# Projecting the dilated values of two chunks between the norm's chunks, with their weights sent among the chunks of x

## The reference

```
def rmsnorm(x, g):
    y = xf * lax.rsqrt(jnp.mean(xf * xf, axis=-1, keepdims=True) + RMS_EPS)
    return (y * g).astype(x.dtype)

def even_mixer(hn, w_in, b_f, w_out, dil_slopes):
    zq, zk, zv, zf, dq, dk, dv = split_cols(hn @ w_in, EVEN_SPLIT)
    log_f = jax.nn.log_sigmoid((zf + b_f).astype(F32)).transpose(0, 2, 1)
    ...
    o_b = dilated_attention(to_heads(dq, 8), to_heads(dk, 8), to_heads(dv, 8), dil_slopes)
    ...

for layer in range(2):
    h = h + mixer(rmsnorm(h, attn_norm[layer]), ...)
    h = h + hierarchical_moe(rmsnorm(h, ffn_norm[layer]), ...)
return rmsnorm(h, final_norm)
```

## Time and profile before

| | us |
|---|---|
| median of 3 runs (lowest to highest) | 1088.04 (1087.25 to 1089.6) |
| span of the profiled execution | 1087.8 |
| PE busy | 999.3 (92%) |
| DVE busy | 387.4 (36%) |
| ACT busy | 228.5 (21%) |
| POOL busy | 91.0 (8%) |
| PE's share of the chain of waits | 66% |
| transfers' share of that chain | 21% |

### The profile page before, as it was taken

The page is one execution under the profiler, slowest core; times in us unless marked ns, Lnnn a source line. Parts: engine busy times, 40 slices in busy tenths (PEclk is TensorE's granted clock), DMA queues, the critical chain, the costliest instruction groups (busy, mean ns, idle before and its releaser), DMA issues.

```text
span 1087.8 us, 12861 instructions
## 1 busy us (share of the span) xinstructions
PE 999.3 (92%) x5140; PEld 575.7 (53%) x5140; DVE 387.4 (36%) x1103; ACT 228.5 (21%) x573; POOL 91.0 (8%) x102
## 2 busy tenths in 40 slices
PE   5999999999998999999778999989999999998866
PEld 3344644455465656666434647536455666665532
DVE  3123721345145333222235217448225333222215
ACT  3113620236021000000012216437111100000002
POOL 2000000000101011111101001000100111111100
PEclk9999999999999999999999999999999999999999
DMA  9522105965336999999999320023634799999996
GB/s 317 213 109 78 78 2 175 211 271 184 115 115 237 406 421 419 420 419 419 419 371 340 156 78 1 11 78 155 239 115 169 283 423 418 420 419 420 418 395 250
DMA packets 64125, 276.95 MB, mean 255 GB/s; under 512 B 12851, under 2 KB 17443, under 8 KB 39994
## 3 DMA queue, kind: packets, MB, share of 16 engines
q1 hardware_dynamic: 53808, 257.48, 61.3%
q0 software_dynamic: 10256, 18.64, 4.9%
HBM read 261.94 MB, written 30.44 MB: 269 GB/s over the span
## 4 chain that ended last, share of the span: by engine, by line
PE 66%; DMA 21%; DVE 5%; issue 4%; SPq 3%; POOL 1%; ACT 0%; POOLq 0%; DVEq 0%
PE bank L855 13%; PE bank L946 10%; PE bank L1069 9%; PE bank L867 9%; DMA K<-rows,small 9%; PE bank L886 6%; PE bank L1083 4%; DMA D<-in_moe_w_down 4%; DMA hnT<-in_moe_w_down 3%; PE bank L900 3%; PE bank L1262 2%; PE bank L916 2%; DMA expert_rows<-K,small 1%; PE bank L980 1%; SPq L454 1%
## 5 line engine op out<-in xcount | busy, mean ns | idle before, releaser
L855 PE MATMUL bank<-hnT,W 128*128 128x512 f32 x336 | 145.1, 593 | 0.8 <-ACT hnT L1356 0.8
L1083 PE MATMUL bank<-D,PT 128*64 128x512 f32 x416 | 102.2, 594 | 10.6 <-DMA D<-in_moe_w_down 9.9
L855 PEld LDWEIGHTS bank<-hnT,W 128*128 128x128 f32 x336 | 63.7, 190 | 80.4 <-issue 79.3
L1069 PE MATMUL bank<-W,PT 128*64 128x256 f32 x640 | 79.0, 388 | 12.4 <-DMA W<-in_moe_w_up 4.9
L1781 DVE SCALAR_TENSOR_TENSOR PT<-bank,small,PT 128x256 f32<-128x256 f32 x32 | 15.5, 484 | 202.6 <-PE bank L1069 202.6
L1803 DVE SCALAR_TENSOR_TENSOR K<-K,small,bank 128x512 f32<-128x512 f32 x64 | 47.8, 747 | 91.8 <-PE bank L1083 91.6
L1069 PE MATMUL bank<-W,cst 128*64 128x256 f32 x640 | 77.2, 380 | 1.8 <-DMA W<-in_moe_w_up 1.8
L1388 ACT ACTIVATE P<-P,nm 128x128 f32<-128x128 f32 (+5 forms) x128 | 68.4, 537 | 30.1 <-DVE nm L1575 29.7
L886 PE MATMUL bank<-K,Q 128*128 128x256 f32 (+3 forms) x256 | 70.4, 417 | 2.2 <-DVE nm L1575 1.0
L867 PE MATMUL bank<-W,hnT 128*128 128x512 f32 (+2 forms) x256 | 71.8, 440 | 0.0
L1069 PEld LDWEIGHTS bank<-W,PT 128*64 128x64 f32 x640 | 52.0, 138 | 32.1 <-issue 12.1
(11 more groups left out here) (241 smaller groups left out, 1358.4 us busy)
## 6 DMA issues: line engine op xcount, KB each, us to landing
D<-in_moe_w_down SPq DMA_DIRECT2D x48, 1024.0 KB, 20.2
W<-in_moe_w_gate SPq DMA_DIRECT2D x40, 1024.0 KB
W<-in_moe_w_up SPq DMA_DIRECT2D x36, 1024.0 KB, 19.9
hnT<-in_moe_w_down SPq DMA_DIRECT2D x12, 1024.0 KB, 17.7
W<-in_e_w_in SPq DMA_DIRECT2D x5, 2048.0 KB
expert_rows<-K SPq DMA_DIRECT2D x2, 4096.0 KB, 34.6
V<-in_moe_w_gate SPq DMA_DIRECT2D x6, 1024.0 KB
Q<-in_moe_w_gate SPq DMA_DIRECT2D x6, 1024.0 KB
```

Of the source, the lines that this page charges most:

```text
L855: last = nc.tensor.matmul(b[:, :], w[:, k, 128 * fb:128 * fb + 128], hnT[:, k, :], start=(k == 0), stop=(k == KD - 1))
L1069: last = nc.tensor.matmul(bank[b][at, 0:256], XT[k // 4][:, k % 4, at], w[:, 256 * k:256 * k + 256], start=(k == 0), stop=(k == KD - 1))
L1083: last = nc.tensor.matmul(bank[5 + half][at, :], hT[:, 128 * c + 64 * a:128 * c + 64 * a + 64], d[:, col:col + 512], start=(c == 0), stop= ...
```

## The change

SP's queue now sends the gain ahead of the small table, and the value weights W2 in two halves of 256 columns, one behind chunk 0 of x and one behind chunk 1. W0 follows whole, then the masks, W1 and W3; W2's old load is gone. POOL issues its three small loads behind the norm, ahead of the position rows. TensorE transposes chunk 0, projects its first 256 value columns, transposes chunk 1, projects the other 256, transposes chunks 2 and 3 and projects the values of chunk 1. The queries follow. The first scores come straight behind the keys, and two value groups follow them. ScalarE and VectorE copy in the new order; ScalarE warms its root with another operand, so that it waits for the table only ahead of the first root; the scratch of the first squares moves from V to P.

```
         junk = flatV[:, 0:1024]
+        first_junk = P[:, 1, 0:1024]
...
         def _(sp):
+            def load_value_half(half):
+                sp.dma_start(W[2][:, :].rearrange("p (k n) -> p k n", k=KD)[:, :, 256 * half:256 * half + 256],
+                             ewin_v[:, :, EVEN_COLS[2] + 256 * half:EVEN_COLS[2] + 256 * half + 256])\
+                  .then_inc((s_half, s_ld["W2"])[half], (16, 48)[half])
             for c in range(C):
                 sp.dma_start(h[:, c, :], x[0, 128 * c:128 * c + 128, :]).then_inc(s_x[c], 16)
                 if c == 0:
-                    sp.dma_start(cst[:, 0:C_MASKS], const_table[:, 0:C_MASKS]).then_inc(s_const, 16)
                     sp.dma_start(gain, attn_norm[0:1, :].partition_broadcast(128).rearrange("a b n -> a (b n)"))\
                       .then_inc(s_gain0, 16)
+                    sp.dma_start(cst[:, 0:C_MASKS], const_table[:, 0:C_MASKS]).then_inc(s_const, 16)
+                if c < 2:
+                    load_value_half(c)
...
-            for half in range(2):
-                sp.dma_start(W[0][:, :].rearrange("p (k n) -> p k n", k=KD)[:, :, 256 * half:256 * half + 256],
-                             ewin_v[:, :, DIL0 + 256 * half:DIL0 + 256 * half + 256])\
-                  .then_inc((s_half, s_ld["W0"])[half], (16, 48)[half])
-            sp.dma_start(cst[:, C_MASKS:C_END], const_table[:, C_MASKS:C_END]).then_inc(s_masks, 16)
...
-            for n in range(1, 4):
+            for n in (0, 1, 3):
                 load_cols(f"W{n}", w_tile(n), ewin_v, EVEN_COLS[n], 512)
-            sp.wait_ge(s_pj, 4)
+                if n == 0:
+                    sp.dma_start(cst[:, C_MASKS:C_END], const_table[:, C_MASKS:C_END]).then_inc(s_masks, 16)
+            sp.wait_ge(s_pj, 6)
...
-            sp.wait_ge(s_pj, 8)
+            sp.wait_ge(s_pj, 10)
...
         def _(pool):
-            pool.dma_start(sinks[:, 0:H], o_sinks[0:1, :].partition_broadcast(128).rearrange("a b n -> a (b n)")
-                           ).then_inc(s_heads, 16)
-            pool.dma_start(bf_sb[:, :], e_b_f.rearrange("a n -> n a")).then_inc(s_heads, 16)
...
-            pool.dma_start(zf_w, ewin_v[:, :, ZF0:ZF0 + H]).then_inc(s_small, 16)
             nc.gpsimd.memset(K[64:128, :, :], 0.0).then_inc(s_kzero, 1)
             pool.wait_ge(s_kzero, 1)
             pool.wait_ge(s_nt, 8)
+            pool.dma_start(zf_w, ewin_v[:, :, ZF0:ZF0 + H]).then_inc(s_small, 16)
+            pool.dma_start(sinks[:, 0:H], o_sinks[0:1, :].partition_broadcast(128).rearrange("a b n -> a (b n)")
+                           ).then_inc(s_heads, 16)
+            pool.dma_start(bf_sb[:, :], e_b_f.rearrange("a n -> n a")).then_inc(s_heads, 16)
             alibi_rows(H)
...
         def _(pe):
-            for c in range(C):
-                transpose_normed(c)
+            def first_values(c):
+                w = w_tile(2)
+                b = group_start()
+                pe.wait_ge(s_ntA, c + 1)
+                pe.wait_ge(s_ntV, c + 1)
+                for half in range(2):
+                    pe.wait_ge(*((s_half, 16), landed("W2", ("even", 2)))[half])
+                    at = slice(256 * half, 256 * half + 256)
+                    for k in range(KD):
+                        last = nc.tensor.matmul(b[:, at], hnT[:, k, 128 * c:128 * c + 128], w[:, k, at],
+                                                start=(k == 0), stop=(k == KD - 1))
+                    if c == 0 and half == 0:
+                        transpose_normed(1)
+                last.then_inc(s_pj, 1)
+            transpose_normed(0)
+            first_values(0)
+            transpose_normed(2)
+            transpose_normed(3)
+            first_values(1)
             norm_ready(0)
             project_features(*even_tile(0), 4)
...
-            project_rows(*even_tile(2), 0, 512, 1, [0])
-            first_scores(DIL, 8, 32)
-            project_rows(*even_tile(2), 0, 512, 1, range(1, C))
+            first_scores(DIL, 10, 32)
+            project_rows(*even_tile(2), 0, 512, 1, range(2, C))
...
         def _(act):
             def norm(v):
+                if v == 0:
+                    act.wait_ge(s_pl, 1)
+                    nc.scalar.activation(warm[:, 0:1], turn[:, 0:1], ACT.Sqrt)
                 for c in range(C):
-                    mean_root(v, c)
-                    if v == 0 and c == 2:
-                        norm_out(0)
+                    squares(v, c)
+                    if v == 0 and c == 0:
+                        act.wait_ge(s_const, 16)
+                    root(v, c)
+                    if v == 0 and c % 2 == 0:
+                        norm_out(c // 2)
...
             norm(0)
+            rows_out(range(2))
             features_out(Q, -0.125, H)
...
-            rows_out()
+            rows_out(range(2, C))
...
         def _(dve):
-            for c in range(C):
-                norm_chunk(0, c)
-                if c >= 2:
-                    norm_out(c - 2)
-            norm_out(C - 2)
-            norm_out(C - 1)
+            norm_chunk(0, 0)
+            norm_out(0)
+            norm_chunk(0, 1)
+            norm_chunk(0, 2)
+            norm_out(1)
+            norm_chunk(0, 3)
+            norm_out(2)
+            norm_out(3)
+            rows_out(range(2))
             features_out(Q, -0.125, H)
```

More of the change, by code:

```diff
@@ L850, in project_features @@
                 for fb in range(blocks):
-                    if ready[0] is s_half and fb == 2:
-                        pe.wait_ge(*landed("W0", ("even", 0)))
                     b = group_start()
@@ L872, in even_tile @@
             def even_tile(n):
-                return w_tile(n), landed(f"W{n % 4}", ("even", n)) if n else (s_half, 16)
+                return w_tile(n), landed(f"W{n % 4}", ("even", n))
             def odd_cols(n, buf):
@@ L1310, in squares @@
                 act.wait_ge(*chunk_ready(v, c))
-                nc.scalar.activation(router_junk if v % 2 else junk, h[:, c, :], ACT.Square, accum_out=ssq[:, c:c + 1]).then_inc(s_sq, 1)
+                nc.scalar.activation(router_junk if v % 2 else junk if v else first_junk, h[:, c, :], ACT.Square, accum_out=ssq[:, c:c + 1]).then_inc(s_sq, 1)
             def root(v, c):
@@ L1322, in norm @@
             def norm(v):
-                nc.scalar.activation(warm[:, v // 2:v // 2 + 1], eps[0:1, 0:1], ACT.Sqrt)
-                for c in range(C):
-                    mean_root(v, c)
-                    if v == 0 and c == 2:
-                        norm_out(0)
+                if v == 0:
+                    act.wait_ge(s_pl, 1)
+                    nc.scalar.activation(warm[:, 0:1], turn[:, 0:1], ACT.Sqrt)
+                else:
+                    nc.scalar.activation(warm[:, v // 2:v // 2 + 1], eps[0:1, 0:1], ACT.Sqrt)
+                for c in range(C):
+                    squares(v, c)
[4 more added lines that the diff above has]
+                        norm_out(c // 2)
                     if v == 2 and c == 0:
@@ L1333, in norm @@
                 if v == 0:
-                    for c in range(1, C):
+                    for c in range(2, C):
                         norm_out(c)
@@ L1376, in features_out, with rows_out @@
                     nc.scalar.activation(dst[0:64, hh, :], b[0:64, :], ACT.Copy, scale=scale).then_inc(s_pjA, 1)
-            def rows_out():
-                for c in range(C):
+            def rows_out(chunks=range(C)):
+                for c in chunks:
                     b = next_group()
@@ L1448, in further_tiles @@
                         hidden_out(over_hT, o_["hte"])
-            act.wait_ge(s_const, 16)
             norm(0)
+            rows_out(range(2))
             features_out(Q, -0.125, H)
```

## The result

The changed kernel takes 1092.41 us (median of 6 runs, 1089.2 to 1095.67) against 1087.73 us for the kernel before in the same comparison: a ratio of 1.0035 [1.0019, 1.0052]. It is slower by about a third of a per cent, and 1087.7 us had been forecast. The profiled execution took 1092.22 us and has a span of 1090.3, so 1.9 us lie outside the span; the span before was 1087.8. So the two profiles are 2.5 us apart, where the medians are 4.7 apart.

The account below looks back on a forecast made before the run. From 19.00 us TensorE alone was taken to bound the kernel. Value work moved ahead gains 1.1 us, the scores' wait loses 1.0; −0.3 taken from 1088.04 gives 1087.7 us, range 1086.0 to 1089.6.

Parts of the forecast that it names:

- the lower end of 7.6: Earliest landing of the small table, in us, taking the table's own lag of 0.8; 8.65 was the landing assumed.
- the 17.3 that I carried over: Time in us when TensorE goes from half to full pace, taken from the trace of the kernel before.
- my second rival: Pace rises late: half pace through the first value half, queries from 33.0 us, 1089.3 us, slower by 1.3; chance 0.18.
- The small loads and the order of the transfers: Start of the kernel: POOL's three small loads moved behind the norm and SP's queue reordered, counted as costing nothing.
- I carry a shift at the first transposes of the probabilities (113.5 us, the end of the last value group) to the end one for one: Behind the first attention: TensorE's progress releases everything, so the start's net shift, −0.3 us, reaches the kernel's end unchanged.
- the sign of being wrong that I had named last: The forecast is wrong if the shift at 113 us doesn't reach the end.
- passes of 160 columns with a weight load each [...] show that loading weights twice as often costs nothing at 256: TensorE's value products: 64 passes in 8.86 us (0.138 each), so halving passes to 256 columns adds no time.
- the net of my sum: 1.1 us gained at the start, 1.0 lost ahead of the first scores: −0.1 to −0.6 us, taken as −0.3.
- The clock theory in its first form: From the reruns: loss behind the head from further half-clock stretches of TensorE, belonging to the changed kernel; 3 to 6 us.
- The load theory: From the experiments: moved small loads or the order of the first transfers cost something later, 3 us or more.

Follow-up runs that it names:

- e1: The changed kernel run once more, unedited: 1092.75 us, ratio 1.0048 [1.0034, 1.0062].
- e3: The kernel before with only the gain sent ahead of the small table and POOL's three small loads issued behind the norm: 1088.3 us, ratio 1.0001.
- e6: The changed kernel with 192 idle waits added among the first query products, 258 instructions later than the kernel before: 1086.73 us, ratio 1.0001.
- e10: The changed kernel with five unread products on x ahead of the first transposes, one behind them, and 160 idle waits: 1083.59 us, ratio 0.9965.
- e9: The changed kernel with 192 idle waits and chunk 2's value group moved ahead of the first scores: 1087.19 us, ratio 1.0000 [0.9987, 1.0014].
- e12: The kernel before with 128 idle waits added among the first query products: 1084.15 us, ratio 0.9974 [0.9965, 0.9984].
- e5: The kernel before with 64 idle waits added among the first query products: 1089.23 us, ratio 1.0027 [1.0004, 1.005].
- e13: The changed kernel with 64 idle waits added among the first query products, 130 instructions later than the kernel before: 1087.22 us, ratio 0.9988.
- e7: The changed kernel with 32 idle waits added among the first query products: 1087.33 us, ratio 1.0004 [0.9988, 1.0021].
- e4: The changed kernel with eight unread products on zeros, six ahead of the first transposes and two behind: 1089.45 us, ratio 1.0016.
- e14: The changed kernel with six unread products on x around the first transposes and 32 idle waits: 1084.57 us, ratio 0.9966 [0.9954, 0.9978].
- e8: The changed kernel with chunk 1's values in 8 products of 512 columns instead of 16 of 256: 1088.48 us, ratio 1.0022.

## Why the prediction was wrong

**The start came out as worked out.** The query groups from 31.6: 31.9 in the chain. An idle of 0.8 ahead of the first scores, released by ScalarE's K: 94.06 to 94.86 in the chain. Last value group ending near 113.2: 113.55. Two errors in it cancel. The first transposes came at 9.52 and not 10.5, since the small table landed 5.81 us after its issue, at 7.47, just under the lower end of 7.6 and not at the 8.65 that I took. And the pace rose about 1 us later than the 17.3 that I carried over: in the records the passes stand 0.43 us apart until about 18.3, and 0.21 behind it. That is the mechanism of my second rival, with an earlier first chunk in the place of its loss. The later pace is no part of the result: the start ends 0.03 us from where it was, and e1, whose pace rose sooner and whose start is 1.2 us ahead of before's, is as slow.

**The small loads and the order of the transfers** I costed at nothing. e3 measures 1.0001 for the small loads, and for the gain ahead of the table; the new order of the weights was not measured alone, but e6 has it and loses nothing.

**The step that failed** is the one that closes the argument: "I carry a shift at the first transposes of the probabilities (113.5 us, the end of the last value group) to the end one for one". I gave as its reason that everything behind is released by TensorE's progress. The shift at 113 us is +0.04 us in the profiles, and the last products come 2.5 us later: the sign of being wrong that I had named last. As a rule of shifts the step is borne out by e10 against e6 (2.67 us at 113 us, 2.91 at the end), while of the 1.35 us that e9 gained nothing is seen at its end. What is wrong is that a shift is all that the head hands on. It hands on its number of instructions as well, and on that I had the term "passes of 160 columns with a weight load each [...] show that loading weights twice as often costs nothing at 256". True for the passes: the second half takes 3.46 us, as forecast (3.43). But the 64 further instructions move every instruction of TensorE that follows to another place in its packets, and this I counted at zero with no bound. The runs put the size of this, for one number of instructions or another, between −0.26% (e12) and +0.48% (e1), −2.8 to +5.2 us on 1088. That is more than the net of my sum, and wider than the whole forecast range of 3.6 us. At 64 to 66 it falls on the worst side seen. No rival had this mechanism.

**What is shown and what is not.** Shown: the loss is of place (how many instructions stand ahead) and not of work, since one like it can be made in the kernel before without work (e5), the loss is taken from the changed kernel without taking work (e6, e13), and another number gives a gain in the kernel before (e12).

For one place the way is visible too: with a packet fetched 0.9 to 1.4 us behind the issue of the output weights, TensorE's wait for them is 1.29 (after), 1.79 (e1), 1.14 (e5), 1.34 (e7), 1.83 (e4) and 0.98 us (e14); in the other ten profiles the wait ahead of that product is 0.69 to 0.92. But that is under 1.2 us; e7 has it without being slower in the end, and e8 is slower without having it. The rest of the loss stands in stretches 2 and 3, where any of the three profiles at 64 and 66 is 2.0 to 7.3 us behind any other, and where transfers of the experts' weights end many of the waits. There a changed wait shows in one kernel and not in the next of the same place (after waits 4.31 us for one tile of down weights that e6 never waits for, but e12 waits 3.53 for it and is faster). Nor is it waits alone: against before, after is busy for longer and idle for less, and against e6 it is 2.3 us longer busy and 3.1 longer idle. Which of the some 40 packets costs what was not taken apart; that the packets act by holding one of the 16 transfer engines is argued from the records and the one place, and not shown for the sum.

The clock theory in its first form falls with e4 and e6, which share the slow start of after, not its loss. Time at half clock in the three stretches is a part of where a profile's time goes, but it doesn't sort the runs: it is 30.7 us in after and e1 and 34.1 in e5, but also 30.7 in e13 and e14 and 34.1 in e9. Whether the packets' place acts through the waits, through the clock or through both was not taken apart. The load theory falls with e3 and e6.

**Net of place the forecast of the change fits**: with the packets back (e6: the same times as before to 0.4 us, up to 375 us) the whole change measures 1.0001 [0.999, 1.0012], that is −1.1 to +1.3 us, against my −0.3 us.

## What to carry to other kernels

When an edit changes how many instructions an engine runs early in a long program, it moves all of that engine's later instruction fetches against the transfers. In this kernel that went with some tenths of a per cent of either sign, so before you credit or blame an edit worth less than that, run it again with idle instructions added until the count is back at its old place, a whole packet on. An early shift on the engine that sets the time can be carried to the end: here 2.7 us from a higher pace of TensorE at its first useful products was, while 1.1 us from a better order (e9) was not seen there.

## What the hardware showed that I had not expected

- **The number of instructions moves the time.** TensorE fetched its program in 41 or 42 packets of 16 KB during the run, about 1 us of one transfer engine each. Idle instructions alone moved the kernel before by +0.27% (64 of them, e5) and −0.26% (128, e12), and 192 of them, with the 66 of the change, brought packets and time back to where they were (e6). The Trainium skill (Runtime: NRT & Kernel Launch, Instruction fetch mechanics) calls the cost of a boundary mostly hidden. That agrees with the size of a fetch, 0.3% of the transfer engines' time in all; if it is the fetches that act here, as is argued above and not shown, their effect is not hidden.
- **Early products raised the pace in one form and not in another.** 12 passes on zeros in 64 rows between 4.57 and 10.06 us left the next products at half pace (e4); 10 passes on x in 128 rows between 4.43 and 9.06 had the first value half at full pace from 11.85 (e10). The two differ in the rows, the values, and where they stand, and which of these counts was not tried.
- **Transposes and the pace.** My forecast weighed the Trainium skill's rule (TensorE: Matmul & The Clock Gate, Part 4: PE-mode transpose) that transposes don't count as busy time. Before, the pace doubled near 17.3 with transposes only the earlier trace rows; after, it rose at about 18.3, and most of what ran ahead of that were products. In e1 it rose sooner than in after, with the same instructions ahead. The runs here speak against the rule, but none was made to isolate it.
